# Three jobs tile by tile behind each norm, squares summed on TensorE, transposes moved, no loops on TensorE

## What is computed

```python
def macaron_ffn(x, g_pre, w_gate, w_up, w_down, g_post):
    n = rms_norm(x, g_pre)
    f = (jax.nn.silu(n @ w_gate) * (n @ w_up)) @ w_down
    return x + 0.5 * rms_norm(f, g_post)

# run_layer
h = macaron_ffn(x, ...ffn1...)                        # 1024 -> 4096 -> 1024
n = rms_norm(h, g_pre); u, v, a, gate = split(n @ w_in, 4)
out_a = u * (tril(W_s) @ layer_norm(v) + b_s)         # chunks of 128 tokens
out_b = silu(layer_norm(causal_dwconv31(a * sigmoid(gate))))
h = h + rms_norm(concat(out_a, out_b) @ w_out, g_post)
q = rms_norm(h, g_pre) @ w_q                          # 4 heads x 256
h = h + rms_norm(softmax(q k / 16) v @ w_o, g_post)   # 256 memory tokens
h = macaron_ffn(h, ...ffn2...)
```

## Time and profile before

| | us |
|---|---|
| median of 3 runs (1690.99 to 1694.79) | 1693.52 |
| the profiled execution | 1697.08 |
| its span, first to last instruction | 1695.3 |
| PE matmuls busy | 1606.7 (95%) |
| DVE busy | 1020.0 (60%) |
| ACT busy | 700.3 (41%) |
| POOL busy | 185.2 (11%) |

### The profile page before, as it was taken

How to read it: one execution, slowest core, us unless ns; L and a number is a source line. 1 busy time by engine, 2 the same in 40 slices (tenths; PEclk the granted TensorE clock), 3 DMA queues, 4 the chain that set the end, 5 groups by cost and what they waited for, 6 DMA issues and landing times.

```text
span 1695.3 us, 28429 instructions
## 1 busy us (share of the span) xinstructions
PE 1606.7 (95%) x11770; PEld 1552.8 (92%) x11770; DVE 1020.0 (60%) x1315; ACT 700.3 (41%) x1204; POOL 185.2 (11%) x167
## 2 busy tenths in 40 slices
PE   6999999999999979999989999789999999999997
PEld 5899999999999979997979769689999999999996
DVE  3863585476367556999344432677367547636744
ACT  4452353255145343642443333445145325415531
POOL 2020120021022000000010010002022012102200
PEclk7999999999999989999989999799999999999997
DMA  4223232233223231223333552023222323322221
GB/s 145 75 75 96 79 100 92 66 94 124 68 83 100 100 107 51 78 98 109 127 120 132 174 175 75 25 75 100 75 83 92 100 76 100 100 75 82 93 76 56
DMA packets 137903, 159.16 MB, mean 94 GB/s; under 512 B 3197, under 2 KB 130769, under 8 KB 137768
## 3 DMA queue, kind: packets, MB, share of 16 engines
q1 hardware_dynamic: 132192, 138.16, 25.5%
q0 software_dynamic: 5488, 19.10, 3.2%
q10 hardware_dynamic: 96, 0.02, 0.0%
HBM read 152.22 MB, written 5.40 MB: 93 GB/s over the span
## 4 chain that ended last, share of the span: by engine, by line
PE 83%; DVE 12%; ACT 3%; issue 1%; DMA 0%; POOL 0%; ACTq 0%; DVEq 0%; POOLq 0%
PE slot L1769 40%; PE slot L1893 37%; DVE f L1573 4%; DVE wp L1202 1%; PE slot L1813 1%; ACT wp L684 1%; PE slot L1827 1%; PE slot L2117 1%; DVE f L1238 1%; PE slot L2136 1%; PE slot L1797 1%; DVE h L1242 1%; DVE f L1282 1%; DVE folded L1217 1%; DVE f L1580 1%
## 5 line engine op out<-in xcount | busy, mean ns | idle before, releaser
L1893 PE MATMUL slot<-nb,wu 128*128 128x288 f32 x4704 | 632.7, 295 | 10.4 <-issue 5.7
L1893 PEld LDWEIGHTS slot<-nb,wu 128*128 128x128 f32 x4704 | 628.4, 188 | 12.6 <-issue 7.9
L1769 PE MATMUL slot<-mid,wp 128*128 128x288 f32 x4176 | 573.1, 298 | 25.7 <-DVE wp L1202 15.1
L1769 PEld LDWEIGHTS slot<-mid,wp 128*128 128x128 f32 x4176 | 563.9, 191 | 31.9 <-issue 24.3
L684 ACT ACTIVATE wp<-raw 128x1024 fp32r<-128x1024 f32 x120 | 127.1, 1059 | 367.3 <-PE slot L1769 340.3
L1202 DVE TENSOR_TENSOR wp<-raw,wp 128x1024 fp32r<-128x1024 f32 x120 | 147.0, 1225 | 138.2 <-ACT wp L684 138.2
L1769 PE MATMUL slot<-n,wp 128*128 128x288 f32 x1152 | 166.4, 306 | 10.8 <-DVE n L1224 10.8
L609 POOL TENSOR_TENSOR raw<-raw,q 128x512 f32<-128x512 f32 x56 | 80.3, 1434 | 873.0 <-DVE wu L1338 561.0
L1769 PEld LDWEIGHTS slot<-n,wp 128*128 128x128 f32 x1152 | 160.7, 196 | 15.0 <-issue 13.6
L1466 DVE TENSOR_TENSOR f<-slot,f 128x576 f32<-128x576 f32 x48 | 36.3, 756 | 134.6 <-PE slot L1769 134.6
L1343 DVE TENSOR_TENSOR wu<-q,wu 128x1024 fp32r<-128x1024 f32 x56 | 88.1, 1572 | 24.6 <-ACT wu L799 23.4
(11 more groups left out here) (245 smaller groups left out, 1416.6 us busy)
## 6 DMA issues: line engine op xcount, KB each, us to landing
raw<-in_ffn_w_gate_dram SPq DMA_DIRECT2D x32, 1024.0 KB, 5.3
raw<-in_ffn_w_up_dram SPq DMA_DIRECT2D x32, 1024.0 KB, 5.4
raw<-in_ffn_w_down_dram SPq DMA_DIRECT2D x32, 1024.0 KB, 4.9
raw<-in_mix_w_in_dram SPq DMA_DIRECT2D x8, 1024.0 KB, 5.4
kring<-in_cache_mem_k_dram POOLq DMA_DIRECT2D x6, 1024.0 KB, 5.4
raw<-in_xattn_w_k_dram SPq DMA_DIRECT2D x4, 1024.0 KB, 4.9
raw<-in_xattn_w_v_dram SPq DMA_DIRECT2D x4, 1024.0 KB, 4.9
raw<-in_mix_w_out_dram SPq DMA_DIRECT2D x4, 1024.0 KB, 5.1
```

What stands on the lines that cost most here:

```text
L1769: ins = pe.matmul(slot(u)[:, half, 0:HALF], wp[:, J % 2, wi, kt], X(xi, kt, half), start=kt == 0 and k == 0, stop=kt == KT - 1 and k == le ...
L1893: ins = pe.matmul(dst[:, 0:HALF], wu[:, p, wi, kt], nb[:, p, xi, kt], start=start and kt == 0 and k == 0, stop=kt == KH - 1 and k == len(P ...
```

## The change

- **Jobs behind a norm.** In a lead-in three jobs go tile by tile: the second one tile behind the first, the third four tiles behind, with its last two tiles behind the spread. For that the weights of jobs 1 and 3 get places of their own (`ffn_x`, `mix_x`, `q_x`), and job 2 takes `wp[:, 1]`. Job 1's are prepared before the last job of the sub-layer ahead has ended, job 2's between the root and the spread of the `post` norm, job 3's between the root and the spread of the `pre` norm.
- **Squares.** VectorE's additions of pairs (L1231) go; TensorE sums each tile's squares, 8 times 4 matmuls in a lead-in where it was 4 times 4. ScalarE's square of tile t waits for the sum of tile t-2.
- **FFN start.** ScalarE and VectorE split B21 and B22 first, and job 3's weights are no longer prepared there.
- **Transposes.** Those of the memory rows (16, with 16 copies on ScalarE) move from ahead of the mixing's lead-in to behind its first four jobs. Those of the memory values (`vtok0`, `vtok1`) and the convolution's state (`glup`, `glus`), ahead of the query's lead-in, move to between the sums and the spread of `post2`; ScalarE's four copies of them stand ahead of its copies to `R`.
- **Keys.** `q_x` lies where `kring[:, 0]` is loaded, so GpSimd loads sample 0's keys behind query job 3.
- **Loops.** TensorE's loop over blocks is written out; the other engines keep theirs.

The diff, cut to its core:

```diff
-    pl.use("post1", "mem0", "mem1", "pre2")
+    pl.use("post1", "pre2")
     pl.job_run("glu0", 4)
-    pl.use("state0", "state1")
+    pl.use("state0", "state1", "mem0", "mem1")
...
-    pl.use("post2", "vtok0", "vtok1", "glup", "glus", "pre3")
+    pl.use("vtok0", "post2", "vtok1", "glup", "glus", "pre3")
...
+        def weights(J):
+            for name, place in NORMED.items():
+                i = J - pl.base[name][0]
+                if i in (1, 3):
+                    return place
+                if i == 2:
+                    return wp[:, 1]
+            return wp[:, J % 2]
...
-            for b in range(NB):
-                if b < 3:
+            for b in (1, 2, 0, 3, 4, 5, 6, 7):
+                if b == 0:
+                    pool.wait_ge(job_done, pl.base["q"][0] + 4)
+                elif b < 3:
                     pool.wait_ge(job_done, pl.base["out"][0] + 1)
...
                     if t >= 2:
-                        act.wait_ge(*normed_to(pre, "added", t // 2))
+                        act.wait_ge(*normed_to(pre, "summed", t - 1))
                     nc.scalar.activation(sq[:, t % 2], h[:, t], ACT.Square).then_inc(sums[pre]["squared"], 1)
-                prepare(pl.base[job][0] + 2)
-                root(pre, D, kind)
+                root(pre, D, kind, lambda: prepare(pl.base[job][0] + 3))
...
             act.wait_ge(qs_zero, 1)
             for t in range(KT):
-                if t:
+                if t >= 2:
                     prepare(pl.base["q"][0] + t + 2)
...
                     take_scaled(sil[:, 1], J0 + 1, u0 + 1)
-                    prepare(J0 + 3)
+                    dve.wait_ge(normed, KT * (STAGE[name] + 1))
+                    b_low(0, nb[:, P2], B21)
+                    b_low(1, nb[:, P3], B22)
                     for e in range(2):
                         scale_gate(name, e)
...
+                for t in range(KT + 1):
                     if t < KT:
                         pe.wait_ge(*normed_to(pre, "ready", t + 1))
+                        part(0, t)
+                    if t:
+                        pe.wait_ge(*normed_to(pre, "squared", t))
+                        sum_tile(pre, t - 1, KT, sq[:, (t - 1) % 2])
+                        part(1, t - 1)
+                    if t >= 4:
+                        part(2, t - 4)
+                part(2, KT - 3)
                 spread_out(pre)
+                part(2, KT - 2)
+                part(2, KT - 1)
+                for i in range(3, count):
                     job(name, i, half_of(src))
...
                 block_of(4, 0)
-                with pe.Fori(1, BLOCKS) as b:
+                for b in range(1, BLOCKS):
                     block_of(0, b)
```

More of the change, by code:

```diff
@@ L296, in build @@
         sums = {}
-        for s, parts in (("pre", ("squared", "recip", "added", "summed", "hi", "ready")),
+        for s, parts in (("pre", ("squared", "recip", "summed", "hi", "ready")),
                          ("post", ("squared", "recip", "added", "scaled", "done"))):
@@ L746, in gates @@
                 for e in range(2):
[L747 removed]
+                    if not ahead:
                         prepare(J + e + 2)
```

211 lines of the change are left out of this document (122 added, 89 removed).

## The result

The changed kernel takes **1704.64 us** (median of 5 runs, 1700.55 to 1707.24) against 1693.04 for the kernel before on the same chip (5 runs): a ratio of 1.0068, interval 1.0046 to 1.0090. It is 11.6 us slower. The prediction said 1694.2 with a range of 1687.5 to 1700.5; the result lies outside it.

A forecast was written before the change was run, and what follows sets the result against it. TensorE, busy 95% of the span, was taken as the bound, leaving only idle and low-clock time to win. Terms +4.1 - 3.2 + 4.6 + 1.5 - 6.3 = +0.7 on 1693.52 gave 1694.2 us, range 1687.5 to 1700.5.

The forecast's parts named there:

- loops: TensorE's written-out block loops: four pauses at block starts go, 6.3 us won.
- the length of a lead-in: In all four stages: the spread starts 24.0 us behind the first matmul, 20.8 of it work at full clock.
- FFN 1: First feed-forward: `R` comes later, job 4 starts 2.1 later and restarts at the low clock (+2.0); 4.1 us slower.
- mixing: Mixing stage: earlier first matmul (2.3 and 0.2) and shorter lead-in (2.6), less 1.9 for the transposes; 3.2 us faster.
- query: Query stage: 3.9 won up to four jobs, then job 4 waits 6.5 for a memset, plus 2.0 low clock; 4.6 slower.
- FFN 2: Second feed-forward: job 4 starts 0.5 us earlier but restarts at the low clock, 2.0; 1.5 us slower.
- Rival 2: Written-out loops pause as often as before, so the 6.3 us are not won: 1700.5; chance 0.11.
- the price of a sum: In each lead-in: one tile's sum of squares on TensorE was taken to cost 0.4 us.
- the gain of 3.9: Query: first matmul 1.8 us earlier, and four jobs done 33.0 behind it instead of 35.1.
- rival 3: Mixing: if VectorE's convolution ends last there, the 3.2 us are lost: 1697.4; chance 0.07.
- Rival 1: Lead-ins and restarts: full clock returns within 3 us of the first matmul, not 6.6: 1687; chance 0.17.
- Rival 4: Third job's weights come late, lead-ins keep their old shape, `R` comes 2.7 earlier, FFNs gain: about 1692; chance 0.03.

The follow-up runs named there:

- e1: Kernel before with only TensorE's loop over blocks 1 to 3 of each feed-forward written out; 1690.75 us against 1693.33, ratio 0.998.
- e3: Changed kernel with GpSimd's zeroing of `qs` moved ahead of the load that waits for query job 3; 1693.52 us against 1693.33 for the kernel before.
- e2: Changed kernel with TensorE's two loops put back; 1717.37 us against 1693.33 for the kernel before, ratio 1.015.
- e11: Changed kernel with early zeroing and glu1's four jobs run as two pairs alternating tile by tile, without waits inside a pair; 1709.46 us, one run.
- e4: Changed kernel with job 4's weights split right behind job 3's in both feed-forwards; 1696.92 us against 1693.33 for the kernel before, ratio 1.0021.
- e5: Changed kernel with e3's edit and, in both feed-forwards, all eight tiles of the third job behind the root's spread; 1684.22 us, ratio 0.9946 to the kernel before.
- e6: Changed kernel with the edits of e3 and e4 together; 1687.49 us against 1692.56 for the kernel before, ratio 0.9969.
- e7: Changed kernel with the edits of e3, e4 and e5 together; 1681.14 us against 1692.56 for the kernel before, ratio 0.9927.

## Why the prediction was wrong

The waits it named were there, each at its place. What failed is the balance: the losses were sized nearly right and the gains too high, above all the loops' gain and the length of a lead-in, which stands in all four stages. Beside each term stands what the stages show, with e1 as the base where loops must be kept out:

```
term      predicted   measured
FFN 1       +4.1      +4.9   (595.54 - 590.61)
mixing      -3.2      -1.75  (mean of nine traces with the change, 252.6, against 254.35 of three without)
query       +4.6      +5.7 to +8.5   (200.19 against 194.45, 194.42 and 191.72)
FFN 2       +1.5      +2.2 to +3.5   (606.13 of e3 and 607.49 against 603.96)
loops       -6.3      -2.6   (e1, by medians)
sum         +0.7      +8.5 to +12.6; by medians +11.6
```

**Loops.** "Four times TensorE pauses at the start of a block, 5.7 in all" was right, and so was what they cost; e1's trace has none. The step that failed is the one that took a pause's removal for the whole effect. In the same trace of before, three of the six looped passes ran their down jobs at 6.24 and not 6.40, 0.93 us for each pass. Measuring the length of the blocks, rather than their pauses alone, would have shown it. The start that lies between the two of the earlier trace rows is

```profile
330.67 1.59 PE L1893 MATMUL slot<-nb,wu 128*128 128x288 f32 x10 [1.53 <-issue]
```

and gives 142.56 and 143.29 between the starts of the blocks in FFN 1, and 141.18 from the last one's start to the end of its last matmul (615.14). In the changed kernel the same three are 141.86, 141.87 and 142.09. Rival 2 (the written-out loops pause too) is excluded by the row at 474.65. e2 adds that the pause itself is no constant: 1.07 to 1.67 at each return of seven loops in four traces, 3.5 and 3.6 at the two of the eighth.

**The length of a lead-in, 24.0.** The spread comes 25.0 (FFN 1), 25.0 (mixing), 26.1 (query) and 25.4 (FFN 2) behind the first matmul: 5.5 more in all, the largest error together. What stands behind the spread was right (9.0 up to the end of four jobs, in the mixing and the query). The step that failed is the price of a sum: 0.4, the length of its row, where e11's section finds 0.55 with what it costs at its edges. For 8 sums that is 1.2, so the work up to the spread is 22.0 and not 20.8. The 3.2 for the first tiles' waiting and the low clock were measured at 3.0 (FFN 1 and mixing), 3.4 (FFN 2) and 4.1 (query). The price enters four times, so adding the terms' bounds as independent made the range too narrow on this side; as independent they give 1690.9 to 1701.2 and not 1689 to 1700. The result lies outside of both.

**Query.** The chain through the memset came as predicted: an idle time of 6.73 (6.5 predicted), and 1.9 for the clock (2.0). e3 proves it, with 8.6 gone for one exchange. The step that failed is the second half of the gain of 3.9. Its first part, the first matmul 1.8 earlier, is there against two of the three traces with the code of before: it comes 8.99 behind the reciprocal of `post2`, where they have 10.76. Against the third, whose clock stayed up, it is 0.9 later (8.09). Its second part rested on four jobs being done 33.0 behind the first matmul; they were done 35.1 behind it (881.22 to 916.3), no earlier than before. Without the stall the stage is 191.59, as long as the second trace of the kernel before and 2.8 shorter than the first. Of that, 1.0 is won behind the four jobs, in all seven traces with the change and without the stall; where is not shown.

**FFNs.** In FFN 1 `R` is ready at 48.16 and job 4 starts at 63.75: 15.6 as predicted. The idle time of 8 to 9 us is there (8.37 and 8.35). The restart at the low clock cost job 4 1.4 in FFN 1 and 2.1 in FFN 2 (25 matmuls in 4.76 and 5.47, where they take 3.32; 2.0 predicted). The term was short by 0.8 in FFN 1 and by 0.7 to 2.0 in FFN 2, by the lead-in's length and, in the changed kernel's own trace, a first matmul of FFN 2 that came 0.9 later than in e3's. e4 and e5 show the two halves of the cause: the third job's tiles put `R` 4.2 later, and job 4's weights stand at the end of VectorE's work behind `R`. The prediction said that job 4 depends on `R` and not on when jobs 2 and 3 are done. It did not draw the conclusion that then the third job ahead of the spread can only cost.

**Mixing.** The four jobs were done 2.5 earlier (661.74 against 664.27) and 4.1 earlier if counted from the end of FFN 1, where 5.1 was predicted. Term by term, over the nine traces with the change and the three without: the first matmul comes 2.2 earlier behind the reciprocal of `post1` (10.5 to 8.2; 2.3 predicted). The lead-in gives 0.9 (35.3 to 34.4) and not 2.6; this is the step that failed. From there to the reciprocal ahead of the second part of the mixing it is 135.7 in all three and 137.4 or 137.5 in eight of the nine: 1.7 for the transposes, 1.9 predicted. A VectorE that ended last there would have swallowed the gain, so this constancy excludes rival 3. Behind that reciprocal the stretch has two lengths, 71.78 or 73.45 before and 71.36 or 73.04 with the change, 0.4 apart at the same length. The two lengths go with TensorE's clock behind one and the same wait of 2.04. It stays up in the first trace of the kernel before (first row). It falls in the changed kernel (second row), but also in the second trace of the kernel before (third row):

```profile
802.00:804.00 2.00, 2.00 (x12) 1.00 0.00 0
```

```profile
802.00:804.00 2.00, 2.00 (x7) 0.50 0.00 0
```

```profile
798.00:800.00 2.00, 2.00 (x9) 0.50 0.00 0
```

So this difference is not the change's: e2, e6 and e7, which have the change, show 71.36. Single traces with the change differ by up to 1.4 us in the whole stage.

**Rival 1** (the clock returns early) did not come about: in the changed kernel the full clock came back 4.6 (FFN 1), 5.6 (mixing), 8.2 (query) and 6.6 (FFN 2) behind a lead-in's first matmul, on average near the 6.6 of the sum and never within the rival's 3. **Rival 4** (the third job is no third job) did not come about, but its number is of interest: it said that the FFNs would gain from it, and e5 shows 8.5 for both.

Three things stay open: why a pass's down jobs run at 6.24 or 6.40, what else the clock's fall hangs on than the wait ahead of it, and why a sum costs more than its row. The squares on TensorE and the moved transposes were not tried each by itself.

## What to carry to other kernels

Before filling an engine's waits with more work, ask what the rest waits for: here six tiles placed ahead of a root filled nothing (0.60 us of waiting without them) and pushed everything that hangs on the root by 4.2 us, twice. When an engine's queue is reordered around a wait, look at what stands behind it on the same engine: one memset behind one load cost 8.6 us. Price a short group of other matmuls by the distance between the starts around it and not by its own row, above all if it stands in the sum 32 times. And read a gain against two executions, or two like stretches, of the old kernel before it is counted: 2.8 of the 6.3 us that I expected from the loops were given back in passes whose pace differs from one execution to the next, and one stage of the kernel before differs by 2.7 between two executions.

## What the runs showed of the hardware

- **A loop's return costs what its place makes it cost.** Pauses of 1.07 to 1.67 us at most returns, 3.4 to 3.6 (1.13 + 2.34, 1.29 + 2.30) where one matmul stood between two pauses; eight instructions more ahead of the loop took 8.9 us off the kernel.
- **The clock falls behind one and the same wait in one execution and not in the next.** Behind 1.59 us of idle time the granted clock was 0.50 in one trace of a kernel and 1.00 in another, and the stage differed by 2.7 us. The Trainium skill, "TensorE: Matmul & The Clock Gate", Part 1, says of the rise of the clock under sustained matmuls that its point varies from run to run because the chip's observation is not tied to the kernel's start. The traces agree and show more of it: in ten traces with the same order in the query's lead-in, the full clock came back 4.2 us behind the first matmul in two (e2, e11) and 8.1 to 8.6 in eight, and four jobs were done 33.3 to 33.4 and 35.0 to 35.3 behind it. That the fall behind a wait has the same reason is not shown.
- **One pass of 288 matmuls takes 37.7 or 38.6 us** with the same instructions at a granted clock of 1.00, 0.130 or 0.133 each, for the pass as a whole, the shorter in 11 of 84 passes.
- **Alternating two jobs every six matmuls costs nothing** (0.134 a matmul over 96), and neither does a wait that is already met (0.140 from start to start at it). **A sum among them costs more than its row:** its 8 matmuls in the rows, 0.38 from their start to the next, make three tiles and a sum 0.55 longer than three tiles (2.96 against 2.41).
